# Zero fill on SP's queue, the first two experts' rows from TensorE, and VectorE's gating straight from PSUM in a routed-expert inference step

## What is computed

```
x = h.reshape(B * S, D)                       # 640 rows
lg = x @ w_rg + b_rg                          # top-1 of 4 groups
le = x @ w_re + b_re                          # then top-2 of 4 experts in it
...
y = 0
for e in range(16):
    a, u = split(x @ w_gu[e], 2)              # 1024 -> 2 x 256
    y = y + comb[:, e:e+1] * ((silu(a) * u) @ w_dn[e])
```

## Time and profile before

| | before |
|---|---|
| median of 3 runs | 735.75 us (734.77 to 741.55) |
| the profiled execution | 734.49 us, of which the span of the trace is 732.7 |
| TensorE matmul busy | 637.9 us, 87% of the span |
| VectorE busy | 337.8 us, 46% |
| ScalarE busy | 174.9 us, 24% |
| GpSimd busy | 133.2 us, 18% |
| moved by DMA | 182.47 MB, mean 249 GB/s |

### The profile page before, as it was taken

How to read it: one execution, slowest core, us unless ns; L and a number is a source line. 1 busy time by engine, 2 the same in 40 slices (tenths; PEclk the granted TensorE clock), 3 DMA queues, 4 the chain that set the end, 5 groups by cost and what they waited for, 6 DMA issues and landing times.

```text
span 732.7 us, 7436 instructions
## 1 busy us (share of the span) xinstructions
PE 637.9 (87%) x2548; PEld 345.0 (47%) x2548; DVE 337.8 (46%) x674; ACT 174.9 (24%) x442; POOL 133.2 (18%) x136
## 2 busy tenths in 40 slices
PE   3899999999996999997899899994599999999900
PEld 2343474345554555576677644442244444444400
DVE  3325463412652554374655636767444323442227
ACT  6000200002221220144655803222011112121113
POOL 1041100131103200020322400112021122222160
PEclk9899999999998999999999999997699999999955
DMA  8989816704586639399932249325999999999166
GB/s 291 387 253 320 321 67 215 275 1 156 45 338 237 242 127 377 143 359 419 421 123 68 93 160 426 125 108 196 264 324 377 359 371 352 356 353 354 74 224 263
DMA packets 64770, 182.47 MB, mean 249 GB/s; under 512 B 5750, under 2 KB 20462, under 8 KB 60644
## 3 DMA queue, kind: packets, MB, share of 16 engines
q1 hardware_dynamic: 44456, 115.59, 45.5%
q10 hardware_dynamic: 15900, 54.01, 19.4%
q0 software_dynamic: 4384, 12.48, 4.9%
HBM read 122.71 MB, written 59.30 MB: 248 GB/s over the span
## 4 chain that ended last, share of the span: by engine, by line
PE 80%; DVE 6%; DMA 4%; issue 3%; ACT 2%; ACTq 2%; POOL 1%; SPq 1%; POOLq 0%; DVEq 0%
PE PS L1520 23%; PE PS L1883 15%; PE PS L1753 9%; PE PS L1899 7%; PE PS L1512 5%; PE PS L1668 4%; PE PS L1551 2%; PE PS L1740 2%; DMA PR<-in_w_ada 2%; ACTq L750 1%; PE PS L1647 1%; PE PS L1461 1%; PE PS L1637 1%; PE PS L1697 1%; PE PS L1542 1%
## 5 line engine op out<-in xcount | busy, mean ns | idle before, releaser
L1520 PE MATMUL PS<-RING,hT 128*128 128x512 f32 x400 | 182.0, 603 | 0.8 <-DVE hT L1019 0.8
L1520 PEld LDWEIGHTS PS<-RING,hT 128*128 128x128 f32 x400 | 74.1, 193 | 87.4 <-issue 86.6
L1883 PE MATMUL PS<-PR,RING 128*128 128x512 f32 x192 | 87.1, 603 | 13.6 <-DVE RING L1401 12.5
L1753 PE MATMUL PS<-RING,hT 128*128 128x512 f32 x160 | 72.7, 600 | 0.0
L1883 PEld LDWEIGHTS PS<-PR,RING 128*128 128x128 f32 x192 | 36.3, 194 | 57.0 <-issue 57.0
L656 POOL TENSOR_TENSOR RING<-RING,hT 128x1024 f32<-128x1024 f32 x8 | 18.8, 2356 | 140.1 <-ACT RING L940 140.1
L1753 PEld LDWEIGHTS PS<-RING,hT 128*128 128x128 f32 x160 | 29.0, 190 | 30.5 <-issue 30.5
L1899 PE MATMUL PS<-PR,TMP 128*128 128x512 f32 x96 | 43.2, 592 | 0.0
L1401 DVE STREAM_TRANSPOSE RING<-RING 128x1024 f32<-128x1024 f32 x16 | 32.1, 2026 | 15.7 <-DMA RING<-scratch_xs 15.4
L1668 PE MATMUL PS<-RING,hT 128*128 128x256 f32 x160 | 36.9, 384 | 0.7 <-ACT TMP L850 0.6
L1512 PE MATMUL PS<-hT,RING 128*128 128x512 f32 (+3 forms) x128 | 35.4, 435 | 0.0
(11 more groups left out here) (319 smaller groups left out, 907.3 us busy)
## 6 DMA issues: line engine op xcount, KB each, us to landing
scratch_xs<-fnorm ACTq DMA_DIRECT2D x16, 2560.0 KB, 16.2
PR<-in_w_gate_up SPq DMA_DIRECT2D x12, 2048.0 KB, 19.7
PR<-in_w_ada SPq DMA_DIRECT2D x20, 1024.0 KB, 10.1
RING<-in_w_in SPq DMA_DIRECT2D x14, 1024.0 KB, 9.0
PR<-in_w_down SPq DMA_DIRECT2D x12, 1024.0 KB, 23.1
RING<-scratch_xs SPq DMA_DIRECT2D x64, 128.0 KB, 12.0
hT<-in_w_gate_up SPq DMA_DIRECT2D x4, 2048.0 KB, 23.0
scratch_xs<-RING ACTq DMA_DIRECT2D x16, 512.0 KB, 11.5
```

Of the source, the lines that this page charges most:

```text
L1520: last = mm(PS[:, bank, :], hTv[:, k, t * P:(t + 1) * P], ring[:, ci % 2, k, :], start=(k == 0), stop=(k == KD - 1))
L1753: last = mm(PS[:, i % 4, :], hTv[:, k, t * P:(t + 1) * P], ring[:, (WOUT + q) % 2, k, :], start=(k == 0), stop=(k == KD - 1))
L1883: last = mm(PS[:, 4 + b, :], xgT[:, b, k, :], gub[s][:, k, :], start=(k == 0), stop=(k == KD - 1))
```

## The change

- SP issues the 16 fills: experts 0 to 3 after `load_mb(3)`, 4 to 6 after `load_mb(7)`, 7 to 11 after `load_mb(9)`, 12 to 15 after `load_rows()`. ScalarE issues none.
- Rows of experts 0 and 1: SP loads them as they are (`xrow`) once tiles 0 to 3 have been scattered; tile 4's scatter waits until these loads have landed. TensorE transposes them, ScalarE copies the result to `xgT`. Tile 4's share is a matmul of its `h2` with a one-hot matrix of ranks (`onehot`), and VectorE adds it to `xgT`. SP's loads for experts 2 and 3 stay as they were, behind tile 4's scatter; the weights of experts 3 and 2 are issued ahead of that wait.
- In the loop VectorE multiplies each PSUM bank with `gate2` into `yo`; ScalarE's copies and GpSimd's products are gone. The transposes of the next pair stand behind the hidden values and ahead of these products; the flags of all rounds are computed ahead of the loop, and VectorE's last quad stands behind its loop.

```diff
+    ZERO_AFTER = {3: (0, 1, 2, 3), 7: (4, 5, 6), 9: (7, 8, 9, 10, 11)}
...
+        def zero_rows(e):
+
+            if e == 0:
+                sp.wait_ge(zero_ready, 1)
+            dst = scratch["xs"][e * T:(e + 1) * T, :].rearrange("(c p) f -> p c f", p=P)
+            sp.dma_start(dst, fnorm[:].unsqueeze(1).broadcast_to([P, NT, D])).then_inc(xs_zeroed, 16)
...
                 load_rows()
+                for e in range(12, NE):
+                    zero_rows(e)
...
                 load_mb(g)
+                for e in ZERO_AFTER.get(g, ()):
+                    zero_rows(e)
...
         sp.wait_ge(x1_ready, 2 * NT)
+        sp.wait_ge(h2_sent[0], 64)
+        sp.wait_ge(h2_sent[1], 32)
+        sp.wait_ge(h2_sent[2], 32)
+        for s in range(2):
+            sp.dma_start(xrow[:, s], scratch["xs"][s * T:s * T + P, :]).then_inc(xq_in[s], 16)
         sp.wait_ge(norm2, NT)
         sp.dma_start(gub[3], w_gu[:, 3]).then_inc(wg_in[3], 16)
-        sp.wait_ge(h2_sent[0], 64)
-        sp.wait_ge(h2_sent[1], 64)
-        sp.wait_ge(h2_sent[2], 32)
-        for s in range(2):
-            load_x(s, s * T)
         sp.wait_ge(lgT_done, NT)
         sp.dma_start(gub[2], w_gu[:, 2]).then_inc(wg_in[2], 16)
+        sp.wait_ge(h2_sent[1], 64)
         for s in range(2, 4):
             load_x(s, s * T)
...
+            if t == NT - 1:
+                for s in range(2):
+                    pool.wait_ge(xq_in[s], 16)
...
-        with pool.Fori(0, n_rounds * QUADS) as qd:
...
-                    nc.gpsimd.tensor_tensor(yo[:, b, :], yo[:, b, :], gate2[b], ALU.mult).then_inc(y_gated, 1)
...
+        for b in range(2):
+            act.wait_ge(first_done, b + 1)
+            for k2 in range(2):
+                ins = nc.scalar.activation(xgT[:, b, 4 * k2:4 * k2 + 4, :],
+                                           PS[:, 2 * b + k2, :].rearrange("p (k s) -> p k s", k=4), ACT.Copy)
+            ins.then_inc(xrow_copied, 1)
...
-                    nc.scalar.activation(yo[:, b, 0:512], PS[:, 2 * b, :], ACT.Copy)
-                    nc.scalar.activation(yo[:, b, 512:D], PS[:, 2 * b + 1, :], ACT.Copy).then_inc(yo_ready, 1)
...
+        dve.wait_ge(rank_done, NT)
+        step(V.tensor_tensor(rank2, PS[:, 7, NE * (NT - 1):NE * (NT - 1) + 2], row0, ALU.subtract))
+        for e in range(2):
+            V.scalar_tensor_tensor(onehot[:, e], misc[:, 64:64 + P], rank2[:, e:e + 1],
+                                   ohb[:, NT - 1, e:e + 1].broadcast_to([P, P]), ALU.is_equal, ALU.mult).then_inc(onehot_ready, 1)
         place(NT - 1)
...
+        for b in range(2):
+            dve.wait_ge(xrow_copied, b + 1)
+            dve.wait_ge(first_done, b + 3)
+            for k2 in range(2):
+                part = xgT[:, b, 4 * k2:4 * k2 + 4, :]
+                last = V.tensor_tensor(part, part, PS[:, (4 if b == 0 else 0) + k2, :].rearrange("p (k s) -> p k s", k=4), ALU.add)
+            last.then_inc(xgT_ready, 1)
+
+        end = dve.value_load(rnd[0:1, 1:2], min_val=QUADS - 1, max_val=ROUNDS * QUADS - 1)
         for b in range(2):
             dve.sem_inc(hid_ready, 1)
...
+        def next_rows(qd, s2):
+
+            for b in range(2):
+                s = (2 * s2 + b + 2) % 4
+                dve.wait_ge(xq_in[s], qd * 64 + (80 if s2 else 64))
+                dve.wait_ge(gu_done[2 * s2 + b], qd + 2)
+                V.transpose(xgT[:, b].rearrange("p k (c j) -> p c k j", c=4),
+                            xq[:, s].rearrange("p c (j k) -> p c k j", k=KD)).then_inc(xgT_ready, 1)
+
+        def gated_out(qd, s2):
+
+            for b in range(2):
+                dve.wait_ge(dn_done[2 * s2 + b], qd + 2)
+                dve.wait_ge(g2_ready, qd * 4 + (2 * s2 + b + 1))
+                dve.wait_ge(yo_stored[b], qd * 32 + (16 * s2 + 16))
+                V.tensor_tensor(yo[:, b, 0:512], PS[:, 2 * b, :], gate2[b][:, 0:512], ALU.mult)
+                V.tensor_tensor(yo[:, b, 512:D], PS[:, 2 * b + 1, :], gate2[b][:, 512:D], ALU.mult).then_inc(yo_ready, 1)
+
+        with dve.Fori(0, end) as qd:
+            for s2 in range(2):
+                gates_of(qd, s2)
+                hidden(qd, s2)
+                next_rows(qd, s2)
+                gated_out(qd, s2)
...
+        for s in range(2):
+            pe.wait_ge(xq_in[s], 16)
+        pe.wait_ge(x1_ready, 2 * NT)
+        for b in range(2):
+            for k in range(KD):
+                last = tr(PS[:, 2 * b + k // 4, (k % 4) * P:(k % 4 + 1) * P], xrow[:, b, k::KD], ident[:])
+            last.then_inc(first_done, 1)
         ranks(NT - 1)
+        pe.wait_ge(x1T_ready, 2 * NT)
+        for b in range(2):
+            pe.wait_ge(onehot_ready, b + 1)
+            if b == 1:
+                pe.wait_ge(xrow_copied, 1)
+            for k in range(KD):
+                last = mm(PS[:, (4 if b == 0 else 0) + k // 4, (k % 4) * P:(k % 4 + 1) * P], h2[(NT - 1) % 3][:, k::KD],
+                          onehot[:, b], start=True, stop=True)
+            last.then_inc(first_done, 1)
         pe.wait_ge(rounds_ready, 1)
```

More of the change, by code:

```diff
@@ L223, in build_body @@
     cnt = sb("cnt", [P, 4])
-    rnd = sb("rnd", [P, 1], I32)
+    rnd = sb("rnd", [P, 2], I32)
     x_loaded = [sem(f"x_loaded{t}") for t in range(NT)]
@@ new lines, in hidden @@
+        def hidden(qd, s2):
+            for b in range(2):
+                dve.wait_ge(sil_ready, qd * 4 + (2 * s2 + b + 1))
+                V.tensor_tensor(hid[:, b], sil[:, b], PS[:, 4 + b, EH:2 * EH], ALU.mult).then_inc(hid_ready, 1)
+                dve.wait_ge(hid_T, qd * 4 + (2 * s2 + b + 1))
+                dve.wait_ge(dn_done[(2 * s2 + b + 2) % 4], qd + (s2 + 1))
+                V.tensor_copy(hidT[:, b], PS[:, 6, 256 * b:256 * b + 256].rearrange("p (k s) -> p k s", k=2)
+                              ).then_inc(hidT_ready, 1)
@@ L1418, in _ @@
+        with dve.Fori(0, end) as qd:
[4 more added lines that the diff above has]
+                gated_out(qd, s2)
+        for s2 in range(2):
+            gates_of(end, s2)
+            hidden(end, s2)
+            if s2 == 0:
+                next_rows(end, s2)
+            gated_out(end, s2)
         for t in range(NT + 1):
@@ L1819, in ranks @@
                     last = mm(PS[:, 6, 80:96], masksb[:, 3, :], ohb[:, j, :], start=(j == 0), stop=(j == NT - 1))
-                last.then_inc(count_done, 1)
+                last.then_inc(rank_done, 1)
         for t in range(NT):
```

96 lines of the change are left out of this document (33 added, 63 removed).

## The result

| | before | after |
|---|---|---|
| median | 736.01 us (734.77 to 741.55, 4 runs) | 727.84 us (726.75 to 732.71, 4 runs) |
| ratio after/before | | 0.99 [0.9862, 0.9938] |
| profiled execution, its span | 734.49, 732.7 us | 727.59, 725.8 us |

The change is worth 8.2 us of the medians and 6.9 of the two spans. The forecast was 18.0 us, and the time lies above the upper end of the range. Where the lead of the new kernel over the old one grows and shrinks is read at points that both traces have. From here on a line number is that of the kernel in whose trace the row stands.

The account below looks back on a forecast made before the run. The prediction held the kernel bound by TensorE's matmuls, with time to win only where TensorE stands still or runs at the low clock. Terms 8.3 + 5.4 + 2.0 + 0 + 2.3 = 18.0 us gave 717.7 us, range 711.5 to 726.

Parts of the forecast that it names:

- the stores of new_C, new_n, new_m, which stay where they are: In the hole term: the slow stretch after 195 us, charged about 9 us more on the drain of the fills.
- The 8.3 us at 227: TensorE's hole at 227 us, waiting for mbuf row 4: wholly regained, 8.3 us, bounds 0 and 8.3.
- The reckoning of the drain itself: Four fills, 10.5 MB leaving SP at about 181.3 us, take 25 us at 421 GB/s, to about 208.
- ScalarE's issues in attention: Units 4 to 8 of attention: moving fill issues from ScalarE to SP saves 5.4 us, bounds 3.5 and 6.5.
- Start of the loop: Gap before the expert loop: early rows save 1.0 us, a raised clock 1.0; together 2.0, bounds -2.2 and +4.7.
- 16 records are 1.7 us at full clock and 3.4 at half: Price of eight float one-hot matmuls of 128 columns before the loop, two records each; two such groups were counted.
- rival 2: Loop start: early rows buy nothing as matmuls run at the low clock; 2.0 turns into -2.2, 722 us; chance 0.12.
- The 1.0 us that a raised clock was to save: At the loop's start 1.95 us were lost to the clock; half may be saved if it is up: 1.0.
- Inside the loop: Expert loop: VectorE takes over the gating products, with slack of about 6 us; 0 for the sum, bounds -1 and +2.
- rival 4: VectorE holds up the expert loop through late row loads, slower than before, 742 us at 3 per pair; chance 0.04.
- Tail: After the last down projection: the store leaves at 697.0 instead of 699.32, saving 2.3 us, bounds 1.8 and 2.6.
- Rival 1: SP's fills block their own queue, mbuf row 4 lands late; 722 us with half the term lost, 726 all; chance 0.20.

Follow-up runs that it names:

- no_new_n: The changed kernel without the store of new_n, which stays unwritten in the output; 713.16 us in its one, profiled run.
- fill_late: The changed kernel with fills later: three after mbuf row 7, five after row 9, eight after load_rows; median 718.63 us, ratio 0.9742.
- three_first: The changed kernel with three fills behind mbuf row 3 instead of four, the fourth behind row 7; 726.13 us in its one, profiled run.
- keep_busy: The changed kernel with five useless matmuls ahead of TensorE's wait for the early rows; median 728.65 us, ratio 0.9827.
- oh_copy: keep_busy plus ScalarE's copy of tile 4's h2 ordered by k, so one-hot weights lie side by side; 724.81 us in its one, profiled run.
- only_fill: The kernel before with nothing but the fill moved to SP on the change's schedule; median 738.53 us, ratio 1.001.
- m_first: The changed kernel with ScalarE's three stores reordered: new_m, then new_C, then new_n; median 722.27 us, ratio 0.979.

## Why the prediction was wrong, and where it was right

**The failed step** is the sentence on "the stores of new_C, new_n, new_m, which stay where they are". I took from the earlier trace rows that they slow the DMA engines, and charged 9 us to the drain of the fill. I did not ask what is queued behind the stores on the engine that issues them, though I asked just that of SP. With 10.5 MB of fills ahead, ScalarE's issue of `new_m` waits until they have drained, and with it the evacuation that TensorE needs: 12.18 us of hole and about 2 at the low clock (4.93 against 3.43 for eight records, and half of 1.11), 14.2 in all, less the 1.4 that TensorE lost at that place before. no_new_n, fill_late and three_first show that it takes both, and how the length follows the fills. The 8.3 us at 227 were indeed regained. By the starts of the mLSTM units' transposes (L1542, L1581), counted from the start of A, the block costs 12.7 us (42.06 us after it, 29.35 before) and the next three units gain 8.8 (29.06 against 37.90 us): together the -3.9 of the stage. The reckoning of the drain itself (25 us, to about 208) was right; it was the very time until which the issue blocked.

The Trainium skill's page DMA: Bandwidth & Descriptors (section Rules for kernel authors) says that a non-contiguous last dimension comes down to one descriptor per element; the store of `new_n` is such a one. No row here counts descriptors, but leaving out this store of 4 KB turned 11.80 us into 1.68.

**ScalarE's issues in attention** (5.4): 5.5. Here the same thing, a long issue while fills are outstanding, was read rightly from the earlier trace rows and priced by TensorE's progress; in all thirteen kernels without fills on ScalarE the stretch from unit 4 to 8 is 19.4 us. That the issue "waits for room in the queue" is a reading, which no run shows. The place 140 us earlier, where the fills would meet other issues of ScalarE, had no such row before.

**Start of the loop** (2.0): -1.1. The rows came when I said (issued 502.67, landed 3.8 us later in the median; the transposes 3.65 us, in the forecast 3.4 to 4.2, whose lower end came from an 0.85 that the earlier trace rows doesn't have). The term that was mis-sized is the one-hot matmuls: "16 records are 1.7 us at full clock and 3.4 at half", so 3.4 or 6.8 for 32; they took 7.88. My rival 2 named that outcome with the wrong cause: the clock. keep_busy gave them the full clock and 7.89 us, oh_copy side-by-side values and 3.81. I had taken the price from transposes of tiles that lie side by side. The Trainium skill's page SBUF — State Buffer (section Door 1: The DMA port swizzle) says that reads that cross to a new 16-byte line with each value pay for it, and puts the free stride at 4 f32; 32 bytes here, and the trace agrees in kind: 336 ns against 192. The 1.0 us that a raised clock was to save in the loop's first pair came to 0.1 here, and to 1.8 in three other executions with the same start: the sum took as settled what differs from one execution to the next.

**Inside the loop** (0, bounds -1 and +2): +3.1 in the two profiled executions. VectorE did not hold up the loop (rival 4): its transposes waited 0.0 us. As executions of kernels with the same loop differ by more than this, the 3.1 are neither an effect shown nor a miss shown.

**Tail** (2.3): 2.3. The output projection's 0.8 was in no term; only_fill has it too, so it came with the move of the fill.

**Rival 1**, the fill in front of its own queue, cost nothing in the changed kernel, and nothing in no_new_n, where the long issue is gone as well. The 3.20 us of hole in m_first are its other condition, the small stores: a bound that showed as soon as the longer one was gone.

## What to carry to other kernels

When a big transfer is moved to another queue, list every DMA that each engine issues while it drains, and what stands behind each issue; behind a store of a few kilobytes in scattered 4-byte pieces the next issue can hold its engine for as long as the transfer lasts. Price a matmul whose weights are strided from rows with strided weights, and let an idle engine put them side by side. Where a stage differs by more between executions than the edit is worth, compare stretches that lie ahead of it, and let medians speak for the rest.

## What the runs showed that I had not expected

- The issue of a store of a few bytes (`new_m`) took 0.52 us with nothing scattered ahead of it, 1.57 to 1.68 in a quiet queue or with `new_n` left out, 7.27 with three fills draining and 11.80 with four; 1.58 in the kernel before, and 11.81 in it with the fills moved (only_fill).
- In f32 matmuls a weight load of 128x128 takes 190 to 192 ns from values side by side and 336 from every eighth. The one-hot matmuls' records then follow every 0.24 us, at either clock, instead of every 0.11, seen at the full clock only. The transposes with weights of the same stride suffered far less: a load took 193 ns against 141 in the mLSTM units' transposes, and 16 of them followed every 0.11 us at the full clock.
- With one and the same code ahead of the expert loop the clock was at 1.00 in the first pair in three executions of seven, and in the other four it fell again: 14.0 us against 15.6 to 15.7.
- The expert loop's DMA rate at a share of 1.03 to 1.04 ranged from 344 to 378 GB/s between executions, and the loop from 168.1 to 180.4 us.
